# The expert loop of a two-block model: the next block's rows are transposed right behind the hidden transposes, inside the second down piece

## The chip, the cores and the metric

The kernel runs on one core of a Trainium2 chip. The metric is the device time of one execution in microseconds (us). The engines are TensorE (PE), VectorE (DVE), ScalarE (ACT), GpSimd (POOL) and SyncE (SP); each works through its own instructions in order, and they meet at semaphores: an instruction may add to a counter when it is done (`then_inc`), and an engine may wait until a counter has reached a value (`wait_ge`).

## The reference

The whole model is a state-space layer, an attention layer, a second block with two kinds of attention, and at its end a mixture of experts over 512 tokens of width 1024. The change lies in the experts:

```python
logits = h @ router_w + router_b          # 32 experts, the 4 best of each token
...
def expert_block(args):                   # 128 rows that go to one expert
    xe, e = args
    gate = jnp.minimum(xe @ w_gate[e] + b_gate[e], SWIGLU_LIMIT)
    up = jnp.clip(xe @ w_up[e] + b_up[e], -SWIGLU_LIMIT, SWIGLU_LIMIT)
    act = (up + 1) * (gate * jax.nn.sigmoid(SWIGLU_ALPHA * gate))
    return act @ w_down[e] + b_down[e]
yb = lax.map(expert_block, (xb, block_e))
```

Each expert has three matrices of 1024 x 1024 in float32. The rows' results are weighted and added up by token.

## The kernel before

**Blocks and pieces.** Tokens are packed into blocks of 128 rows of one expert. The number of blocks depends on the routing; here it is 35. A loop on each engine runs over all blocks but the last, which is written out behind it. A block reads 12 MB of weights, in 12 pieces of 1 MB (`PIECES`), q = 0 to 11: two gate pieces, two up pieces, again two gate and two up pieces for the second half of the hidden width, and four down pieces, q = 8 to 11.

**Exact products.** A float32 number is split into a high part that TensorE takes at full speed, and the low rest. A product is three matmuls: high by high, high by low, low by high (`exact_product`, L262 to L264). ACT makes the high part of each piece (`take_high`, L2988), DVE subtracts it from the raw piece to get the low part (`take_low`, L2992). There are four buffers for high parts, so ACT works `AHEAD` = 3 pieces ahead: in step q it waits until PE has used piece q - 1 (`used`), then rounds piece q + 3, which from q = 9 on is a piece of the next block.

**A block on PE.** PE waits for the block's rows (`x_ready`, L3133), takes pieces 0 to 7 (`open_products`, 12 matmuls of 512 columns each), and pieces 8 to 11 (`down_products`, 12 matmuls each: j = 0, 1 times two column halves times three). The inner activations come out of ACT and DVE with rows on the partitions; PE transposes them, four 128 x 128 transposes a half (`turn_hidden`, L3086): the first half behind piece 5, the second in the middle of piece 9. ACT and DVE then split them into high and low (L3198, L3266), and piece 10 waits for the second half's split (`hidden_split`).

**The next block's rows.** POOL gathers 128 rows of tokens into `x_rows` (`gather_rows`). PE transposes them by eight 128 x 128 transposes into banks 4 and 5 (`turn_rows`, L2973), ACT copies them out rounded (`take_x_high`, L2981), and DVE subtracts (`take_x_low`, L2984), which gives `x_ready`. In ACT's order the copy stands behind the rounding of step q = 10:

```python
for q in range(PIECES):
    of_piece(b, q, True)
    if q == 10:
        act.wait_ge(x_turned, b + 2)
        take_x_high()
```

DVE's order is alike: in step q it subtracts piece q + 3, and `take_x_low` stands behind step 10. In step 9 DVE has the hidden split (L3266) and the next block's piece 0, in step 10 the next block's piece 1.

SP loads the weight pieces in order; each load waits until PE has used the same piece of the block before.

Of the kernel before, what the change touches and what calls it, by code (L numbers as in the profile page):

```python
# [258 lines left out]
def exact_product(nc, out, left, right, start, stop):  # L259


    nc.tensor.matmul(out, left[0], right[0], start=start, stop=False)  # L262
    nc.tensor.matmul(out, left[0], right[1], start=False, stop=False)  # L263
    return nc.tensor.matmul(out, left[1], right[0], start=False, stop=stop)  # L264
# [2659 lines left out]
def experts(k, e, stored):  # L2924
# [32 lines left out]
    def number_left_out(engine):  # L2957
        return engine.value_load(plan[0:1, 2 * NP + 1:2 * NP + 2], min_val=0, max_val=NBLK - NE)

    def last_block(engine):  # L2960
        return engine.value_load(plan[0:1, 2 * NP + 2:2 * NP + 3], min_val=NE - 1, max_val=NBLK - 1)

    def block_number(engine, turn, left_out):
        return nc.s_assert_within(engine.snap((turn - left_out - 1) & 63), 0, NBLK - 2,
                                  skip_runtime_bounds_check_because="only turns above the number left out come here")
# [5 lines left out]
    def turn_rows():  # L2971
        for d in range(DT):
            i = nc.tensor.transpose(k.psum[:, 4 + d // 4, (d % 4) * P:(d % 4 + 1) * P], e["x_rows"][:, d * P:(d + 1) * P],  # L2973
                                    k.cst("ident"))
        i.then_inc(x_turned, 1)
# [18 lines left out]
    with nc.Block() as block:  # L2994
        @block.sync
        def _(sp):
            n = number_of_blocks(sp)
            with sp.Fori(1, NBLK) as b:
                with sp.If(b < n):
                    expert = sp.value_load(plan[0:1, bass.ds(b, 1)], min_val=0, max_val=NE - 1)  # L3000
                    for q in range(PIECES):

                        sp.wait_ge(used, PIECES * b + (q + 2 - PIECES))
                        load_expert_piece(k, e, sp, q, expert)
            sp.wait_ge(last_staged, 4)
            for t in range(ST):
                sp.dma_start(sums[:, t, :], k.sums_dram[t * P:(t + 1) * P, :]).then_inc(sums_in[t], 16)
            for c, t in units:
                if t == ST - 1:
                    sp.wait_ge(added_pool, c + 1)  # L3010
                else:
                    sp.wait_ge(added_dve, (ST - 1) * c + t + 1)
                sp.dma_start(k.io["out"][t * P:(t + 1) * P, c * NB:(c + 1) * NB], half(k.resid[:, t, :], c)).then_inc(stored, 16)
            sp.wait_ge(stored, 16 * len(units))
# [60 lines left out]
        @block.tensor  # L3075
        def _(pe):
            left_out = number_left_out(pe)
            pe.wait_ge(x_in, 16)
            nc.tensor.transpose(k.psum[:, 0, 0:P], k.cst("ident"), k.cst("ident")).then_inc(used, 1)
            turn_rows()  # L3080

            def turn_hidden(b, h):

                pe.wait_ge(hidden_ready, 2 * b + h + 1)
                for f in range(4):
                    i = nc.tensor.transpose(k.psum[:, 2 * h, f * P:(f + 1) * P], e["gate"][:, (4 * h + f) * P:(4 * h + f + 1) * P],  # L3086
                                            k.cst("ident"))
                i.then_inc(hidden_turned, 1)

            def open_products(b, q):  # L3090
                pe.wait_ge(low_ready, PIECES * b + (q + 1))
                r = q // 2
                w = [x.rearrange("p (d f) -> p d f", d=4) for x in (high[q % NHI], low[q])]
                for j in range(4):
                    d = 4 * (q % 2) + j
                    x = [t[:, d * P:(d + 1) * P] for t in (e["x_high"], e["x_low"])]
                    i = exact_product(nc, k.psum[:, r, :], x, (w[0][:, j, :], w[1][:, j, :]), start=(d == 0), stop=False)
                if q % 2 == 1:
                    if q == 1:
                        pe.wait_ge(chosen, b + 1)  # L3100
                    at = (r % 2) * D + (r // 2) * NB
                    i = nc.tensor.matmul(k.psum[:, r, :], e["choice"], e["bias"][:, at:at + NB], start=False, stop=True)  # L3102
                return i

            def down_product(q, j, c):
                f = 2 * (q - 8) + j
                x = [t[:, f * P:(f + 1) * P] for t in (e["hidden_high"], e["hidden_low"])]
                w = [x.rearrange("p (f c) -> p f c", f=2) for x in (high[q % NHI], low[q])]
                return exact_product(nc, k.psum[:, 6 + c, :], x, [t[:, j, c * NB:(c + 1) * NB] for t in w],
                                     start=(f == 0), stop=(f == DT - 1))  # L3110

            def down_waits(b, q):
                pe.wait_ge(low_ready, PIECES * b + (q + 1))
                if q == 8:
                    pe.wait_ge(y_ready, b + 1)
                if q % 2 == 0:
                    pe.wait_ge(hidden_split, 2 * b + ((q - 8) // 2 + 1))

            def down_products(b, q):
                down_waits(b, q)  # L3120
                for j in range(2):
                    for c in range(2):
                        i = down_product(q, j, c)
                    if q == 9 and j == 0:
                        turn_hidden(b, 1)
                return i

            with pe.Fori(0, NBLK // GROUP) as g:
                with pe.If(left_out < GROUP * g + (GROUP - 1)):
                    with pe.Fori(0, GROUP) as i:  # L3130
                        with pe.If(left_out < GROUP * g + i):
                            b = block_number(pe, GROUP * g + i, left_out)
                            pe.wait_ge(x_ready, b + 1)  # L3133
                            for q in range(8):
                                open_products(b, q).then_inc(used, 1)
                                if q == 5:
                                    turn_hidden(b, 0)
                            for q in range(8, PIECES):
                                down_products(b, q).then_inc(used, 1)
                                if q == 9:  # L3140
                                    pe.wait_ge(x_in, 16 * b + 32)
                                    turn_rows()

            last = last_block(pe)
            pe.wait_ge(x_ready, last + 1)
            for q in range(8):
                open_products(last, q).then_inc(used, 1)
                if q == 5:
                    turn_hidden(last, 0)
            for q in range(8, PIECES - 1):  # L3150
                down_products(last, q).then_inc(used, 1)
            down_waits(last, PIECES - 1)
            for c in range(2):
                for j in range(2):
                    i = down_product(PIECES - 1, j, c)
                i.then_inc(y_done, 1)

            def add_biases(c, t):
                for n in range(2):
                    at = n * D + c * NB  # L3160
                    nc.tensor.matmul(k.psum[:, bank_of(c, t), :], e["spread_t"][:, t * P:(t + 1) * P], e["bias"][:, at:at + NB],  # L3161
                                     start=(n == 0), stop=False)

            def spread_rows(c, t):
                to = e["onehot"][:, t * P:(t + 1) * P]
                nc.tensor.matmul(k.psum[:, bank_of(c, t), :], to, half(y_high, c), start=False, stop=False)
                nc.tensor.matmul(k.psum[:, bank_of(c, t), :], to, half(y_low, c), start=False, stop=True).then_inc(product, 1)

            for t in range(ST):
                add_biases(0, t)  # L3170
            pe.wait_ge(onehot_ready, ST)
            pe.wait_ge(y_low_ready, 1)
            for t in range(ST):
                spread_rows(0, t)
            for t in range(ST):
                if t >= 2:
                    pe.wait_ge(y_gated, t - 1)
                add_biases(1, t)
            pe.wait_ge(y_low_ready, 2)
            for t in range(ST):  # L3180
                spread_rows(1, t)
# [325 lines left out]
```

## Time and profile before

| | |
|---|---|
| median of 3 runs | 3100.88 us (3095.59 to 3105.14) |
| the profiled execution: its own time | 3099.18 us |
| its span in the trace | 3097.3 us |
| PE busy | 2926.6 us, 94% |
| DVE busy | 2052.1 us, 66% |
| ACT busy | 1593.9 us, 51% |
| expert loop, first to last row transposes | 1820.6 to 3028.6 us of the span |

The rows below are read as follows. Times are in us from the start of the span. A line such as L2988 is a line of the kernel. PE is matmuls, PEld is TensorE's weight loads. A matmul's end is modelled, so the distances of starts are what one reads on PE. "x4" is the number of instructions merged into a row. `[0.71 <-PE banks L264]` means that the engine was idle for 0.71 us and was released by PE's L264. The granted clock (PEclk) is 1.00 at 2.4 GHz and 0.50 at 1.2 GHz.

### The profile page before, as it was taken

The page shows a single profiled execution, that of the slowest core. Times are in us where ns is not written, and L with a number is a line of the kernel's source. Part 1 is how long each engine was busy: PE and PEld are TensorE (multiplying, and loading weights), DVE is VectorE, ACT ScalarE, POOL GpSimd, SP SyncE. Part 2 cuts the span into 40 slices and gives each one's busy share as a digit, 9 for nine tenths or more (in the row PEclk, how much of TensorE's full clock was granted, in tenths as well). Part 3 has the DMA queues.
Part 4 walks back from the last instruction along what each step waited for, and adds up shares of the span by engine and source line. Part 5 has one row for each costly group of instructions (what it writes and reads, how often), then busy time and mean ns, then how long its engine had stood idle before and what let it go on. Part 6 is the DMA issues. An engine that isn't in the chain of part 4 may idle for free. (4 is left out here: it accounts for less than half of the span.)

```text
span 3097.3 us, 42024 instructions
## 1 busy us (share of the span) xinstructions
PE 2926.6 (94%) x15072; PEld 2339.9 (76%) x15072; DVE 2052.1 (66%) x2363; ACT 1593.9 (51%) x1731; POOL 562.3 (18%) x480
## 2 busy tenths in 40 slices
PE   7889999997999999899999869999999999999997
PEld 3668888764688888776677768888888888888886
DVE  8451223657632236745653479999999999999998
ACT  4242222334632224434542247777777777777774
POOL 1002200021212100003101102332222322222225
PEclk9899999997999999999999879999999999999999
DMA  6512222212022322111013369999999999999994
GB/s 241 223 70 82 109 95 109 86 43 102 15 109 82 122 82 103 40 49 47 1 41 109 128 228 378 381 382 389 388 386 381 377 388 386 391 383 380 383 388 157
DMA packets 87918, 637.74 MB, mean 206 GB/s; under 512 B 10400, under 2 KB 10848, under 8 KB 25024
## 3 DMA queue, kind: packets, MB, share of 16 engines
q1 hardware_dynamic: 77584, 598.79, 49.6%
q0 software_dynamic: 9936, 36.75, 4.4%
q8 instruction: 77, 1.26, 0.2%
q10 hardware_dynamic: 288, 0.67, 0.1%
q14 instruction: 33, 0.27, 0.0%
HBM read 610.38 MB, written 25.79 MB: 205 GB/s over the span
## 5 line engine op out<-in xcount | busy, mean ns | idle before, releaser
L2992 DVE TENSOR_TENSOR arena_rounded<-arena,arena_rounded 128x2048 fp32r<-128x2048 f32 x420 | 960.9, 2309 | 94.5 <-ACT arena_rounded L2988 94.5
L2988 ACT ACTIVATE arena_rounded<-arena 128x2048 fp32r<-128x2048 f32 x420 | 801.5, 1918 | 210.4 <-PE banks L264 136.4
L262 PE MATMUL banks<-arena_rounded,operand_rounded 128*128 128x512 f32 (+1 forms) x2064 | 822.5, 399 | 14.0 <-DVE small_rounded L3266 8.1
L263 PE MATMUL banks<-arena_rounded,operand_rounded 128*128 128x512 f32 (+1 forms) x2064 | 806.2, 391 | 0.0
L264 PE MATMUL banks<-arena_rounded,operand_rounded 128*128 128x512 f32 (+1 forms) x1504 | 585.6, 389 | 0.0
L262 PEld LDWEIGHTS banks<-arena_rounded,operand_rounded 128*128 128x128 f32 x2064 | 391.3, 190 | 94.7 <-DVE arena_rounded L2992 8.9
L263 PEld LDWEIGHTS banks<-arena_rounded,operand_rounded 128*128 128x128 f32 x2064 | 391.4, 190 | 77.6 <-issue 1.0
L264 PEld LDWEIGHTS banks<-arena_rounded,operand_rounded 128*128 128x128 f32 x1504 | 284.5, 189 | 59.5
L262 PE MATMUL banks<-operand_rounded,arena_rounded 128*128 128x512 f32 (+2 forms) x712 | 267.2, 375 | 6.0 <-PE banks L264 5.3
L263 PE MATMUL banks<-arena_rounded,arena_rounded 128*128 128x512 f32 (+1 forms) x688 | 266.0, 387 | 0.0
L264 PE MATMUL banks<-operand_rounded,arena_rounded 128*128 128x512 f32 (+2 forms) x712 | 263.7, 370 | 0.0
L263 PE MATMUL banks<-operand_rounded,arena_rounded 128*128 128x512 f32 (+2 forms) x712 | 263.5, 370 | 0.0
L251 DVE TENSOR_TENSOR arena_rounded<-arena,arena_rounded 128x2048 fp32r<-128x2048 f32 x33 | 75.6, 2292 | 272.7 <-ACT arena_rounded L247 272.7
L262 PE MATMUL banks<-arena_rounded,arena_rounded 128*128 128x512 f32 (+1 forms) x608 | 236.6, 389 | 4.6 <-PEq L1369 2.3
L762 DVE TENSOR_TENSOR arena_rounded<-arena,arena_rounded 128x2048 fp32r<-128x2048 f32 x36 | 82.5, 2291 | 238.2 <-ACT arena_rounded L709 238.2
L264 PE MATMUL banks<-arena_rounded,arena_rounded 128*128 128x512 f32 (+1 forms) x608 | 235.1, 387 | 0.0
L264 PE MATMUL banks<-arena_rounded,small_rounded 128*128 128x512 f32 x560 | 220.7, 394 | 0.0
L709 ACT ACTIVATE arena_rounded<-arena 128x2048 fp32r<-128x2048 f32 x34 | 65.1, 1915 | 216.4 <-PE banks L264 212.1
L930 POOL TENSOR_TENSOR arena<-small 128x512 f32<-128x512 f32 x64 | 75.7, 1183 | 502.9 <-ACT small L916 257.5
L262 PEld LDWEIGHTS banks<-operand_rounded,arena_rounded 128*128 128x128 f32 (+1 forms) x712 | 133.8, 188 | 36.0 <-issue 13.6
L264 PEld LDWEIGHTS banks<-operand_rounded,arena_rounded 128*128 128x128 f32 (+1 forms) x712 | 133.8, 188 | 23.6
L263 PEld LDWEIGHTS banks<-operand_rounded,arena_rounded 128*128 128x128 f32 (+1 forms) x712 | 133.9, 188 | 23.4 <-issue 1.0
(493 smaller groups left out, 3969.0 us busy)
## 6 DMA issues: line engine op xcount, KB each, us to landing
arena<-in_gate SPq DMA_DIRECT2D x140, 1024.0 KB, 7.7
arena<-in_up SPq DMA_DIRECT2D x140, 1024.0 KB, 7.7
arena<-in_down SPq DMA_DIRECT2D x140, 1024.0 KB, 5.7
arena<-in_dense SPq DMA_DIRECT2D x62, 2048.0 KB, 7.7
arena<-in_dense SPq DMA_DIRECT2D x6, 1024.0 KB, 4.9
small<-in_rows SPq DMA_DIRECT2D x7, 512.0 KB, 7.5
expert_sums<-operand SPq DMA_DIRECT2D x5, 512.0 KB, 5.1
resid<-in_x SPq DMA_DIRECT2D x4, 512.0 KB, 6.8
```

The lines of the kernel that those rows point to most:

```text
L251: self.nc.vector.tensor_tensor(low, raw, high.bitcast(F32), ALU.subtract).then_inc(done, 1)
L262: nc.tensor.matmul(out, left[0], right[0], start=start, stop=False)
L263: nc.tensor.matmul(out, left[0], right[1], start=False, stop=False)
L264: return nc.tensor.matmul(out, left[1], right[0], start=False, stop=stop)
L709: nc.scalar.activation(w_high, raw, ACT.Copy).then_inc(high, 1)
L762: V.tensor_tensor(w_low, raw, w_high.bitcast(F32), ALU.subtract).then_inc(low, 1)
L930: nc.gpsimd.tensor_tensor(hidden[:, n, :], relu[:, n % 2, :], relu[:, n % 2, :], ALU.mult).then_inc(squared, 1)
L2988: nc.scalar.activation(high[q % NHI], raw[:, q, :], ACT.Copy).then_inc(high_ready, 1)
L2992: nc.vector.tensor_tensor(low[q], raw[:, q, :], high[q % NHI].bitcast(F32), ALU.subtract).then_inc(low_ready, 1)
```

## The change

The eight row transposes and the wait on the gathered rows are moved from behind piece 9 into its middle, right behind the four transposes of the hidden activations. The six matmuls of j = 1 of piece 9 now follow them. The last block, which has no next one, calls the same function without them.

```diff
-            def down_products(b, q):
+            def down_products(b, q, ahead):
                 down_waits(b, q)
                 for j in range(2):
                     for c in range(2):
                         i = down_product(q, j, c)
                     if q == 9 and j == 0:
                         turn_hidden(b, 1)
+                        if ahead:
+                            pe.wait_ge(x_in, 16 * b + 32)
+                            turn_rows()
                 return i
...
                             for q in range(8, PIECES):
-                                down_products(b, q).then_inc(used, 1)
-                                if q == 9:
-                                    pe.wait_ge(x_in, 16 * b + 32)
-                                    turn_rows()
+                                down_products(b, q, True).then_inc(used, 1)
...
-                down_products(last, q).then_inc(used, 1)
+                down_products(last, q, False).then_inc(used, 1)
```

The signal `used` of piece 9 hangs on the last matmul that the function returns. On PE, at the middle of piece 9 inside the loop, this is the first piece of the difference in PE's instructions; L3086 are the hidden transposes, L3127 is the wait on the gathered rows, L2973 the row transposes, L262 to L263 the first matmuls of j = 1:

```order
 L3084 REGISTER_ALU
 L3086 MATMUL banks<-const,operand 128x128 x4
+L3127 ISA
+L2973 MATMUL banks<-const,arena 128x128 x8
 L262 MATMUL banks<-arena_rounded_56,operand_rounded_49 128x512
 L263 MATMUL banks<-arena_rounded_54,operand_rounded_49 128x512
```

The row transposes came in ahead of the six matmuls of j = 1. At the end of piece 9 on PE, six matmuls on, they are gone; the last L264 shown carries the signal `used` in both kernels, and L3113 belongs to the first product of piece 10:

```order
 L263 MATMUL banks<-arena_rounded_54,operand_rounded_49 128x512
 L264 MATMUL banks<-arena_rounded_56,small_rounded_59 128x512
-L3141 ISA
-L2973 MATMUL banks<-const,arena 128x128 x8
 L3113 REGISTER_ALU
 L262 MATMUL banks<-arena_rounded_57,operand_rounded_49 128x512
```

The signal's matmul moved behind the transposes. The instructions of DVE, ACT, POOL and SP are the same in both kernels and stand in the same order.

## Rows read from the trace of the kernel before

**Rows 1.** The page: busy time, share of the span and instructions of each engine.
```profile
PE 2926.6 (94%) x15072; PEld 2339.9 (76%) x15072; DVE 2052.1 (66%) x2363; ACT 1593.9 (51%) x1731; POOL 562.3 (18%) x480
```

**Rows 2.** One turn of the loop: length, busy times, granted clock, DMA share, GB/s.
```profile
2389.08:2424.57 35.49, 35.49 (x166) 29.39 (x164) 32.80 (x22) 26.92 (x19) 9.80 (x7) 1.00 1.01 384
```

**Rows 3.** Waits in the expert stage: us in total, times, longest.
```profile
PE banks L262 <- DVE small_rounded L3266: 8.1, 2, 5.4
PE banks L262 <- DVE operand_rounded L2984: 3.1, 1, 3.1
...
DVE arena_rounded L2992 <- ACT arena_rounded L2988: 81.7, 99, 1.6
...
POOL expert_sums L3049 <- ACT operand L3229: 421.4, 34, 12.4
```

**Rows 4.** Row transposes; and who waited for DVE's L2984 (us, times).
```profile
L2973 PE MATMUL banks<-const,arena x280: 270/273/421, 1820.6 to 3028.6; 128*128 128x128 f32 x140
...
  PE banks L262: 3.1, 1
```

**Rows 5.** Timeline of PE in piece 9: start, duration, line, operation.
```profile
2422.50 0.40 PE L264 MATMUL banks<-arena_rounded,small_rounded 128*128 128x512 f32 x1
...
2423.41 0.39 PE L263 MATMUL banks<-arena_rounded,operand_rounded 128*128 128x512 f32 x1
...
2424.33 0.40 PE L264 MATMUL banks<-arena_rounded,small_rounded 128*128 128x512 f32 x1
...
2425.67 0.39 PE L263 MATMUL banks<-arena_rounded,operand_rounded 128*128 128x512 f32 x1
```

**Rows 6.** Timeline of ACT around the row copy L2981, and one earlier rounding.
```profile
2413.18 1.91 ACT L2988 ACTIVATE arena_rounded<-arena 128x2048 fp32r<-128x2048 f32 x1
...
2424.77 1.92 ACT L2988 ACTIVATE arena_rounded<-arena 128x2048 fp32r<-128x2048 f32 x1 [0.71 <-PE banks L264]
2426.59 1.01 ACT L2981 ACTIVATE operand_rounded<-banks 128x1024 fp32r<-128x1024 f32 x1
2428.39 1.92 ACT L2988 ACTIVATE arena_rounded<-arena 128x2048 fp32r<-128x2048 f32 x1 [0.79 <-PE banks L264]
```

**Rows 7.** Timeline of DVE around the row subtraction L2984, and one earlier subtraction.
```profile
2415.12 2.29 DVE L2992 TENSOR_TENSOR arena_rounded<-arena,arena_rounded 128x2048 fp32r<-128x2048 f32 x1 [0.50 <-ACT arena_rounded L2988]
...
2424.32 0.68 DVE L3266 TENSOR_TENSOR small_rounded<-banks,operand_rounded 128x512 fp32r<-128x512 f32 x1
2424.93 4.48 DVE L2992 TENSOR_TENSOR arena_rounded<-arena,arena_rounded 128x2048 fp32r<-128x2048 f32 x2
2429.33 1.21 DVE L2984 TENSOR_TENSOR operand_rounded<-banks,operand_rounded 128x1024 fp32r<-128x1024 f32 x1
```

**Rows 8.** Timeline at the border of two blocks.
```profile
2430.68 0.39 PE L264 MATMUL banks<-arena_rounded,small_rounded 128*128 128x512 f32 x1
2430.69 0.19 PEld L262 LDWEIGHTS banks<-arena_rounded,operand_rounded 128*128 128x128 f32 x1
...
2431.14 0.39 PE L263 MATMUL banks<-arena_rounded,operand_rounded 128*128 128x512 f32 x1
...
2431.19 0.69 ACT L3228 ACTIVATE operand<-banks,arena 128x512 f32<-128x512 f32 x1 [0.89 <-PE banks L264]
```

**Rows 9.** Timeline where PE really waited for DVE: before the loop, last block.
```profile
1824.13 1.23 DVE L2984 TENSOR_TENSOR operand_rounded<-banks,operand_rounded 128x1024 fp32r<-128x1024 f32 x1
...
1825.62 0.29 PEld L262 LDWEIGHTS banks<-arena_rounded,operand_rounded 128*128 128x128 f32 x1 [3.47 <-issue]
...
3073.64 0.68 DVE L3266 TENSOR_TENSOR small_rounded<-banks,operand_rounded 128x512 fp32r<-128x512 f32 x1
...
3074.44 0.19 PEld L262 LDWEIGHTS banks<-arena_rounded,operand_rounded 128*128 128x128 f32 x1 [3.11 <-DVE arena_rounded L2992]
...
3074.78 0.40 PE L263 MATMUL banks<-arena_rounded,operand_rounded 128*128 128x512 f32 x1
```

**Rows 10.** Busy times, clock after the 3.1 us wait (columns as in rows 2).
```profile
1825.00:1829.40 4.40, 3.78 (x9) 3.01 (x10) 2.14 (x2) 1.91 (x1) 1.28 (x3) 0.50 0.40 123
```

## The prediction

> **What bounds the kernel now.** I read the totals first, then the expert loop, then the waits in it, then one block instruction by instruction. The totals show TensorE (PE) busy 94% of the span and VectorE (DVE) 66% [rows 1], but that is an average over all stages. The edit touches only the expert loop, so I took one turn of it, from one set of row transposes to the next: 35.49 us, in which PE is busy all 35.49 us at a granted clock of 1.00, that is 2.4 GHz, and DVE 32.80 us [rows 2]. The list of waits says the same for the whole loop: from its first block on PE waited only three times, 3.1 us once (before the first block) and 8.1 us twice (in the last block) [rows 3]. In every turn between, PE ran one matmul behind the other, and DVE waited 81.7 us for ScalarE (ACT) [rows 3]. So PE sets the time, and a change can shorten the loop only by making PE's own stream shorter. It can lengthen it by making PE wait for something that so far came just in time. The reader should therefore look for what comes just in time.
>
> The row transposes run once before the loop and once in each of its 34 turns: 280 of them in eights are 35 sets [rows 4]. So whatever happens per turn counts 34 times; the 34th is what the last block's start waits for.
>
> **The part that only moves.** In the profiled turn the matmul before the four hidden transposes starts at 2422.50 and the second matmul behind them at 2423.41: 0.91 us. The same two points around the eight row transposes are 2424.33 and 2425.67: 1.34 us [rows 5]. Four more transposes cost 0.43 us, 0.108 each; eight added to a set that exists already cost 0.86 us, where a set of eight alone costs 1.34 - 0.46 = 0.88 (the 0.46 is two matmul pitches: 2431.14 - 2430.68 = 0.46, one 0.23 [rows 8]). Joining the two sets saves PE some 0.02 us a turn, 34 x 0.02 = 0.7 us in all, if nothing else happened. The wait on the gathered rows moves with them; it stands between two transposes now, where less work covers the instruction itself. No row shows a stand-alone wait between transposes. From below it is 0, which I take, since PE is fed ahead of its array; from above it is the 0.07 us that such a wait costs on ACT, whose L3228 starts 2431.19 - 2430.68 = 0.51 us behind the matmul that it waits for [rows 8], where a rounding without it starts 0.44 us behind (below). The gather itself is not late: GpSimd (POOL) comes to it in its own order, behind the 421.4 us that it waits for the block's output in the loop [rows 3], so that an earlier end of the transposes starts nothing earlier on it either.
>
> **The part that becomes late.** The signal that down piece 9 is used up goes with that piece's last matmul. Before, this matmul started at 2424.33, ahead of the row transposes; now the eight transposes stand ahead of its last six matmuls, so it starts 0.86 us later, at 2425.19. Follow who waits for it.
>
> ACT's rounding of the next block's second piece started at 2424.77, 0.44 us behind that matmul, and took 1.92 us [rows 6]. Now: 2425.19 + 0.44 = 2425.63, ending at 2427.55 in place of 2426.69. ACT's copy of the transposed rows (L2981) stands behind it in ACT's order. The transposes are ready earlier than before, but this copy starts later, about 2427.45 to 2428.46. ACT's next rounding started at 2428.39 [rows 6], behind an idle time, so ACT has caught up there.
>
> DVE's subtraction of that second piece is the second half of the pair that starts at 2424.93 and lasts 4.48 us. One takes 2.28, so the second started at 2427.13 [rows 7], 0.44 us after the rounding had ended: DVE had its own backlog, and this is the cover. The new end of the rounding, 2427.55, passes it. With the 0.03 us that DVE needs behind ACT (a rounding ended at 2413.18 + 1.91 = 2415.09 and the subtraction behind it started at 2415.12 [rows 6, 7]) the subtraction starts at 2427.58, 0.45 us later than before. DVE's row subtraction L2984 stands right behind it: it ran from 2429.33 to 2430.54 [rows 7] and now ends at 2430.99. Its own input from ACT, 2428.46, is in time.
>
> L2984 is what PE waits for at the head of each block. PE began to load that block's first weights at 2430.69, 0.01 us behind the start of the matmul before [rows 8], so nothing held it, but L2984 had ended only 0.15 us earlier. How long does PE need when it really waits? In the last block, DVE ended at 3073.64 + 0.68 = 3074.32 and PE loaded at 3074.44: 0.12 us; before the first block, for this very wait, DVE ended at 1825.36 and PE loaded at 1825.62: 0.26 us [rows 9]. The loop's own 0.15 us without a hold says that 0.12 to 0.15 is enough in the steady state, 0.26 being the upper bound. So of 0.45 us of lateness only 0 to 0.03 are covered.
>
> A late start gives something back. When PE restarts from idle, the second matmul came 3074.78 - 3074.44 = 0.34 us after the load [rows 9]; in the stream it is 2431.14 - 2430.69 = 0.45 [rows 8]. So 0.11 us are recovered. The new time of the second matmul is 2430.99 + 0.15 + 0.34 = 2431.48, against 2431.14: **0.34 us a turn**; with 0.12 it is 0.31, with 0.26 it is 0.45. PE's saving of 0.02 does not count any more, since PE waits at the end of this path anyway. The delay does not heal: the next block's chain on ACT and DVE is again started by PE's signals, and the 0.45 us arise anew.
>
> **The sum.** 34 x 0.34 = 11.6 us (0.31: 10.5; 0.45: 15.3). The profiled execution took 3099.18 us, its span 3097.3. 3099.2 + 11.6 = 3110.8. The median of the runs before, 3100.88, is 1.7 higher; from there it is 3112.5. I say 3112. With the moved wait exposed (0.07) on top it is 34 x 0.41 = 13.9, and with the 0.26 as well 34 x 0.52 = 17.7 us.
>
> A rule stands against holding the load back. The Trainium skill, page TensorE: Matmul & The Clock Gate, section Step-by-step: what each phase is for, says that TensorE pulls weight loads ahead of matmuls in flight. Here the weights are the rows that are late, and in [rows 9] the load starts at 1825.62, behind L2984's end and not ahead of it, so the trace shows no pull-ahead over the wait. By the rule the restart would save another 0.11 us a turn, and the sum would be about 8 us; its chance is part of the second rival's.
>
> **The rivals.**
> - *The cover holds, and only the saving is left* (not slower). One mechanism: DVE's backlog at piece 9 is longer in most turns than in the one I read, so that the rounding, though 0.86 us late, is still in time. It decides from 0.86 us of cover; the profiled turn has 0.44. For it: PE gets rid of one change between matmuls and transposes. Against it: L2984 never held PE in the loop [rows 4], and 34 turns without a wait of PE leave it little room to differ from one turn to the next. Time: 3099.2 - 0.7 = 3098.5 by the profile, 3100 by the median.
> - *Half the lateness is absorbed.* The 0.44 us from matmul to rounding shrinks, or the restart recovers more than 0.11. With 0 us from DVE's end to PE's load, the least that can be, the turn costs 2430.99 + 0.34 - 2431.14 = 0.19 us: 6.5 us, 3106 to 3107.
> - *The down pieces stall too.* The next wait of PE behind the set, for the split of the hidden rows, is met at 2424.32 + 0.68 = 2425.00 by DVE [rows 7]. PE's first load for that piece falls at 2425.20 now. 0.20 us is above the 0.12 us needed, by 0.08. If ACT or DVE slip by 0.2 us there, it costs 0.12 us x 34 = 4 us more: 3116.
> - *The short stops cost the clock.* PE would stand still once a turn for some 0.4 us. Before the first block PE was idle for 3.1 us and then ran 4.40 us at a granted clock of 0.50 (1.2 GHz) [rows 10]. If each stop did that, 34 x 2.2 = 75 us: 3174. The stops here are an eighth of that one, and the turn with its transposes runs at clock 1.00 throughout [rows 2]. The Trainium skill, same page, section A second HAM failure mode: psum-queue depth-cycling, names short idles between groups of matmuls as such a cause; no row of this kernel shows it for a stop this short.
>
> **How the numbers follow.** The head-of-block wait as summed: 0.70. Half absorbed: 0.10. Cover holds or nothing changes: 0.10. Down pieces stall too: 0.07. Clock: 0.03. The range 3104 to 3119 takes in the 3106 of the half-absorbed case and the 17.7 us of the upper bounds, and leaves out the holding cover and the clock. A measurement of this kernel tells about 0.3%, 9.3 us, from no change: 3110.2 is the border. My value lies only 2 us beyond it, so part of the likeliest case falls on this side. Slower: three quarters of 0.70, the down pieces, the clock: 0.63. Same: the rest of it and the two milder cases, less a little: 0.33. Faster: 0.04.
>
> **What would show it.** In the profile after, the turn is 35.8 to 35.9 us in place of 35.49; the list of waits shows PE waiting for DVE L2984 some 33 times more, in small pieces; ACT's idle time before the rounding ahead of L2981 is about 1.57 us in place of 0.71; DVE is idle some 0.4 us before the second subtraction of each pair; the set of twelve transposes is one piece on PE. If L2984 never appears as PE's releaser, the chain above is wrong. If it appears but for 0.1 us, the cover or the restart was mis-sized. If the granted clock is below 1.00 in the loop, the last rival has come true.

## The result and the profile after

The changed kernel's median is 3111.84 us over 13 runs; the kernel before, run beside it each time, has 3098.38 over 13. The ratio of the two is 1.0047, with a 95% interval of 1.0035 to 1.0058: slower, by 11 to 18 us. One of the changed kernel's thirteen runs took 3727.78 us at a mean granted clock of 0.74, where every other run of either kernel beside it lies at 3123.09 us or below; the ratio leaves it out, the median of the other twelve is 3111.0, and since it left no trace, whether the change has to do with it is not shown. The profiled execution has a span of 3108.3 us, against 3097.3.

The page of the changed kernel answers to [rows 1], and the row of one turn of the loop, here from one row subtraction L2984 to the next, to [rows 2]:

```profile
PE 2933.5 (94%) x15072; PEld 2337.3 (75%) x15072; DVE 2055.3 (66%) x2363; ACT 1593.1 (51%) x1731; POOL 577.6 (19%) x480
...
2434.13:2470.01 35.88, 35.77 (x166) 29.38 (x165) 32.90 (x22) 26.93 (x20) 10.47 (x7) 1.00 1.00 380
```

The turn went from 35.49 to 35.88 us with the same instructions and the clock still at 1.00. These are single turns. From here on "the turn" of a kernel is the mean distance of two starts of L2984 (L2985 where the lines are shifted) over the 33 turns behind the first: 35.87 us here, 35.49 before, 0.38 us more.

The timeline of the changed kernel, all engines, from the matmul ahead of the hidden transposes to the head of the next block (the answer to [rows 5 to 8]):

```profile
2426.83 0.40 PE L264 MATMUL banks<-arena_rounded,small_rounded 128*128 128x512 f32 x1
...
2427.06 0.60 PE L3086 MATMUL banks<-const,operand 128*128 128x128 f32 x4
...
2427.50 1.04 PE L2973 MATMUL banks<-const,arena 128*128 128x128 f32 x8
...
2428.61 0.39 PE L263 MATMUL banks<-arena_rounded,operand_rounded 128*128 128x512 f32 x1
2428.66 0.69 DVE L3266 TENSOR_TENSOR small_rounded<-banks,operand_rounded 128x512 fp32r<-128x512 f32 x1
...
2429.54 0.39 PE L264 MATMUL banks<-arena_rounded,small_rounded 128*128 128x512 f32 x1
...
2429.54 0.19 PEld L262 LDWEIGHTS banks<-arena_rounded,operand_rounded 128*128 128x128 f32 x1
...
2429.97 1.92 ACT L2988 ACTIVATE arena_rounded<-arena 128x2048 fp32r<-128x2048 f32 x1 [1.58 <-PE banks L264]
...
2431.79 1.01 ACT L2981 ACTIVATE operand_rounded<-banks 128x1024 fp32r<-128x1024 f32 x1
...
2431.92 2.29 DVE L2992 TENSOR_TENSOR arena_rounded<-arena,arena_rounded 128x2048 fp32r<-128x2048 f32 x1 [0.38 <-ACT arena_rounded L2988]
...
2434.13 1.22 DVE L2984 TENSOR_TENSOR operand_rounded<-banks,operand_rounded 128x1024 fp32r<-128x1024 f32 x1
...
2434.98 0.39 PE L264 MATMUL banks<-arena_rounded,small_rounded 128*128 128x512 f32 x1
...
2435.48 0.19 PEld L262 LDWEIGHTS banks<-arena_rounded,operand_rounded 128*128 128x128 f32 x1 [0.53 <-issue]
...
2435.82 0.40 PE L263 MATMUL banks<-arena_rounded,operand_rounded 128*128 128x512 f32 x1
```

Read it from the first row, 2426.83, as zero; before, the same point is 2422.50 [rows 5].

| behind the last matmul ahead of the hidden transposes, us | before | after | later by |
|---|---|---|---|
| last matmul of piece 9 (carries `used`) | 1.83 | 2.71 | 0.88 |
| ACT's rounding of the next block's second piece | 2.27 | 3.14 | 0.87 |
| DVE's subtraction of that piece | 4.63 | 5.09 | 0.46 |
| end of DVE's row subtraction L2984 | 8.04 | 8.52 | 0.48 |
| PE's load of the first weights of the next block | 8.19 | 8.65 | 0.46 |
| second matmul of the next block | 8.64 | 8.99 | 0.35 |

PE loads 0.13 us behind L2984's end, 0.50 us behind the start of the matmul before, where it was 0.01 us in [rows 8]. It does so at all 34 heads behind the first: the load stands 0.12 to 0.13 us behind L2984's end and 0.47 to 0.50 us behind the start of the matmul before. So the head of the block is where the time goes.

The rest of the 0.38 us is a slower start behind the hold: from the second matmul of the block to the first L3102, 23 matmuls on, it is 5.25 us here, 5.21 before; the medians over the 34 heads are 5.24 and 5.22. The far row in the changed kernel (the near one, 2435.82, stands above):

```profile
2441.07 0.39 PE L3102 MATMUL banks<-arena_rounded 128*128 128x512 f32 x1
```

And before, the row at the far end (the near one, 2431.14, is in [rows 8]):

```profile
2436.35 0.39 PE L3102 MATMUL banks<-arena_rounded 128*128 128x512 f32 x1
```

### The profile page after: what moved, and what is told of

It reads as the page before. It is cut to its first block and busy times, and to the rows that moved or that the text cites. A ratio compares the mean times of both kernels' runs of the same rounds, so it can differ in the third digit from the quotient of the medians.

```text
span 3108.3 us, 42024 instructions
## 1 busy us (share of the span) xinstructions
PE 2933.5 (94%) x15072; PEld 2337.3 (75%) x15072; DVE 2055.3 (66%) x2363; ACT 1593.1 (51%) x1731; POOL 577.6 (19%) x480
## 5 line engine op out<-in xcount | busy, mean ns | idle before, releaser
L262 PE MATMUL banks<-arena_rounded,operand_rounded 128*128 128x512 f32 (+1 forms) x2064 | 823.4, 399 | 18.3 <-DVE small_rounded L3266 8.4
L263 PE MATMUL banks<-arena_rounded,operand_rounded 128*128 128x512 f32 (+1 forms) x2064 | 806.1, 391 | 0.0
L264 PE MATMUL banks<-arena_rounded,operand_rounded 128*128 128x512 f32 (+1 forms) x1504 | 586.1, 390 | 0.0
L262 PEld LDWEIGHTS banks<-arena_rounded,operand_rounded 128*128 128x128 f32 x2064 | 391.0, 189 | 113.0 <-issue 25.6
L263 PEld LDWEIGHTS banks<-arena_rounded,operand_rounded 128*128 128x128 f32 x2064 | 391.4, 190 | 77.4 <-issue 1.0
L264 PEld LDWEIGHTS banks<-arena_rounded,operand_rounded 128*128 128x128 f32 x1504 | 284.6, 189 | 60.1
L262 PE MATMUL banks<-operand_rounded,arena_rounded 128*128 128x512 f32 (+2 forms) x712 | 267.9, 376 | 6.0 <-PE banks L264 5.2
L263 PE MATMUL banks<-arena_rounded,arena_rounded 128*128 128x512 f32 (+1 forms) x688 | 266.7, 388 | 0.0
L264 PE MATMUL banks<-operand_rounded,arena_rounded 128*128 128x512 f32 (+2 forms) x712 | 264.5, 371 | 0.0
L263 PE MATMUL banks<-operand_rounded,arena_rounded 128*128 128x512 f32 (+2 forms) x712 | 264.3, 371 | 0.0
L262 PE MATMUL banks<-arena_rounded,arena_rounded 128*128 128x512 f32 (+1 forms) x608 | 237.4, 390 | 4.6 <-PEq L1369 2.3
L264 PE MATMUL banks<-arena_rounded,arena_rounded 128*128 128x512 f32 (+1 forms) x608 | 235.6, 387 | 0.0
L264 PE MATMUL banks<-arena_rounded,small_rounded 128*128 128x512 f32 x560 | 219.9, 393 | 0.0
L262 PEld LDWEIGHTS banks<-operand_rounded,arena_rounded 128*128 128x128 f32 (+1 forms) x712 | 134.5, 189 | 35.9 <-issue 13.6
L264 PEld LDWEIGHTS banks<-operand_rounded,arena_rounded 128*128 128x128 f32 (+1 forms) x712 | 134.6, 189 | 23.5
L263 PEld LDWEIGHTS banks<-operand_rounded,arena_rounded 128*128 128x128 f32 (+1 forms) x712 | 134.6, 189 | 23.4 <-issue 1.0
```

## The experiments

The theory: the signal `used` of piece 9 is late, so ACT's rounding is late, so DVE's subtraction is late beyond its cover of 0.44 us, so L2984 behind it is late, and PE holds. The first rival: the new place costs PE itself (twelve transposes in a row, a switch in the middle of piece 9, the wait between transposes). The second: ACT's late row copy L2981 holds L2984.

### Only the rounding is late

PE's instructions are those of the kernel before, in the same order. Only ACT changes:

```diff
                             for q in range(PIECES):
+                                if q == 10:
+                                    act.wait_ge(x_turned, b + 2)
                                 of_piece(b, q, True)
                                 if q == 10:
-                                    act.wait_ge(x_turned, b + 2)
                                     take_x_high()
```

> The kernel before, with its row transposes at their old place and TensorE's instructions untouched; only ScalarE now waits for the end of the row transposes ahead of its rounding of the next block's second piece, where it waited for the end of piece 9. If the lateness of this rounding is the cause: the rounding starts 0.98 us later (0.75 us from the start of a set of four transposes to ScalarE's answer, 0.43 more for eight, against 0.20 after their start before), DVE's row subtraction ends 0.57 us later, and the turn grows by 0.43 us at the block's head and some 0.03 in the matmuls behind the restart, to 35.95 us; 34 turns give about 15 us, 3113 to 3115. If the place of the transposes on TensorE is the cause (twelve in a row, or the wait between them), the turn stays at 35.49 us and the time at that of the kernel before.

Measured: 3116.36 us median over 5 runs, against 3096.25 over 15 of the kernel before, ratio 1.0064 (1.0050 to 1.0077); turn 36.00 us, 0.05 above what was expected: the row subtraction came 0.6 us late in place of 0.57, and the rounding 1.01 in place of 0.98. The timeline of this kernel at the same places:

```profile
2394.45 0.40 PE L264 MATMUL banks<-arena_rounded,small_rounded 128*128 128x512 f32 x1
...
2397.73 1.92 ACT L2988 ACTIVATE arena_rounded<-arena 128x2048 fp32r<-128x2048 f32 x1 [1.71 <-PE banks L2973]
...
2399.69 2.29 DVE L2992 TENSOR_TENSOR arena_rounded<-arena,arena_rounded 128x2048 fp32r<-128x2048 f32 x1 [0.52 <-ACT arena_rounded L2988]
2401.90 1.22 DVE L2984 TENSOR_TENSOR operand_rounded<-banks,operand_rounded 128x1024 fp32r<-128x1024 f32 x1
...
2403.24 0.19 PEld L262 LDWEIGHTS banks<-arena_rounded,operand_rounded 128*128 128x128 f32 x1 [0.64 <-issue]
...
2403.25 0.49 PE L262 MATMUL banks<-arena_rounded,operand_rounded 128*128 128x512 f32 x1 [0.22 <-DVE operand_rounded L2984]
```

The rounding starts 3.28 us behind the reference point (the last matmul ahead of the hidden transposes, here 2394.45), 1.01 later than before, and PE's first load comes 0.12 us behind L2984's end at 2403.12. A wait on ACT alone, with the transposes where they were, makes the turn longer by more than the change does, 0.51 against 0.38 us. The first rival falls as the main cause. In this kernel the list of PE's waits names L2984 in every turn:

```profile
PE banks L262 <- DVE operand_rounded L2984: 10.6, 35, 3.1
```

### The rows ahead of the rounding and the subtraction

The changed kernel; the transposes stay in the middle of piece 9, and ACT and DVE take the rows first. On DVE, and alike on ACT:

```diff
                             for q in range(PIECES):
-                                of_piece(b, q, True)
                                 if q == 10:
                                     dve.wait_ge(x_high_ready, b + 2)
                                     take_x_low()
+                                of_piece(b, q, True)
```

> The changed kernel, with ScalarE's row copy ahead of the rounding of the next block's second piece, and DVE's row subtraction ahead of its subtraction of that piece. If the chain used, rounding, subtraction, row subtraction is the cause: the row subtraction ends some 2 us before TensorE needs it, the head of a block has no hold, and the turn is 35.48 us, TensorE's own stream; time as before the change, within 0.1%. If the place of the transposes costs TensorE itself, the turn stays at 35.87 us and the time near 3112.

Measured: 3096.76 us median over 11 runs, against the same 3096.25, ratio 0.9998 (0.9989 to 1.0007); turn 35.46 us. The whole loss is gone with the twelve transposes in place. Timeline of this kernel:

```profile
2421.84 0.40 PE L264 MATMUL banks<-arena_rounded,small_rounded 128*128 128x512 f32 x1
...
2423.59 1.03 ACT L2981 ACTIVATE operand_rounded<-banks 128x1024 fp32r<-128x1024 f32 x1 [0.17 <-PE banks L2973]
2424.98 1.92 ACT L2988 ACTIVATE arena_rounded<-arena 128x2048 fp32r<-128x2048 f32 x1 [0.37 <-PE banks L264]
...
2426.48 1.22 DVE L2984 TENSOR_TENSOR operand_rounded<-banks,operand_rounded 128x1024 fp32r<-128x1024 f32 x1
2427.61 2.28 DVE L2992 TENSOR_TENSOR arena_rounded<-arena,arena_rounded 128x2048 fp32r<-128x2048 f32 x1
```

L2984 ends 5.86 us behind the reference point, where PE's load of [rows 8] stands at 8.19. The rounding is as late as in the changed kernel (3.14), and it does no harm: what costs the time is the row subtraction that stood behind it.

### Four or six of the eight transposes in the middle

```diff
-                            turn_rows()
+                            turn_rows(0, 4)
...
                                 down_products(b, q, True).then_inc(used, 1)
+                                if q == 9:
+                                    turn_rows(4, DT)
```

> The changed kernel with four of the eight row transposes in the middle of piece 9 and four behind it. The signal of piece 9 is 0.43 us late and DVE's cover is 0.44 us: by the chain the second subtraction starts at most 0.02 us later, the head has no hold, the turn is 35.49 to 35.52 us. If what counts is that transposes stand in the middle at all (the wait, the switch), the turn grows by at least half of 0.38, to 35.68.

> The changed kernel with six of the eight row transposes in the middle of piece 9 and two behind it. By the chain: 0.65 us late less 0.44 of cover and plus 0.03 gives 0.25 us at the row subtraction, of which the spare 0.02 and the 0.11 of the restart go off: 0.11 us at the head, 0.03 behind it, turn 35.61 to 35.63 us. If the cost goes with the number of transposes moved, three quarters of 0.38: 35.77 us.

Measured, one run each: turn 35.51 us and 3100.14 us with four; turn 35.64 us and 3103.21 us with six. The 15 runs of the kernel before beside them reach from 3093.23 to 3103.74, so these two are read by their turns and not by their times. In both, these lines are one number on (L2989 is the rounding, L2993 the subtraction, L2985 the row subtraction). With four:

```profile
2422.90 0.40 PE L264 MATMUL banks<-arena_rounded,small_rounded 128*128 128x512 f32 x1
...
2425.60 1.92 ACT L2989 ACTIVATE arena_rounded<-arena 128x2048 fp32r<-128x2048 f32 x1 [1.12 <-PE banks L264]
...
2425.34 4.51 DVE L2993 TENSOR_TENSOR arena_rounded<-arena,arena_rounded 128x2048 fp32r<-128x2048 f32 x2
2429.76 1.22 DVE L2985 TENSOR_TENSOR operand_rounded<-banks,operand_rounded 128x1024 fp32r<-128x1024 f32 x1
```

DVE's two subtractions are still one piece: the cover has just held. L2985 ends 8.08 us behind the reference point, 0.04 later than before, which uses up PE's spare time; the turn is 0.02 us longer. With six there is a gap of 0.15 us, and a hold:

```profile
2423.95 0.40 PE L264 MATMUL banks<-arena_rounded,small_rounded 128*128 128x512 f32 x1
...
2426.87 1.92 ACT L2989 ACTIVATE arena_rounded<-arena 128x2048 fp32r<-128x2048 f32 x1 [1.35 <-PE banks L264]
...
2428.82 2.29 DVE L2993 TENSOR_TENSOR arena_rounded<-arena,arena_rounded 128x2048 fp32r<-128x2048 f32 x1 [0.15 <-ACT arena_rounded L2989]
...
2432.37 0.19 PEld L262 LDWEIGHTS banks<-arena_rounded,operand_rounded 128*128 128x128 f32 x1 [0.26 <-issue]
```

All kernels in which ACT and DVE keep their order give one curve of the turn over the start of the rounding behind the reference point:

| kernel | rounding starts at | turn |
|---|---|---|
| before | 2.27 | 35.49 |
| four in the middle | 2.70 | 35.51 |
| six in the middle | 2.92 | 35.64 |
| the change (eight) | 3.14 | 35.87 |
| before, rounding held on ACT | 3.28 | 36.00 |

It is nearly flat up to 2.70, and from 2.92 on it rises by 0.23 in 0.22 us and by 0.13 in 0.14: one for one. A cost that goes with the number of transposes moved would have put four of them at 35.68 and six at 35.77.

### One side at a time, and the wait

Only ACT's copy ahead, or only DVE's subtraction ahead, by the half of the edit above that belongs to it:

> The changed kernel with only ScalarE's row copy moved ahead of the rounding of the next block's second piece; DVE's order as it was. The copy fits into ScalarE's idle time of 1.58 us, the rounding still starts when piece 9 is used up, DVE still subtracts that piece first: the turn stays at 35.87 us. If instead the late row copy (0.8 us later than before the change) is what holds the row subtraction, the turn falls back to 35.49.

> The changed kernel with only DVE's row subtraction moved ahead of its subtraction of the next block's second piece; ScalarE's order as it was. The row copy ends about 5.97 us behind the last matmul ahead of the hidden transposes, the row subtraction 1.25 us later, 1 us before TensorE needs it: no hold, turn 35.48 us. If the ScalarE side is the bound, the turn stays at 35.87 us.

Measured: with ACT alone, turn 35.87 us, one run of 3107.71 us; with DVE alone, turn 35.46 us, one run of 3095.52 us, where a single run of the kernel before beside both took 3100.53. Here too the turns decide. The rows of DVE with ACT's order alone changed:

```profile
2430.87 2.29 DVE L2992 TENSOR_TENSOR arena_rounded<-arena,arena_rounded 128x2048 fp32r<-128x2048 f32 x1 [0.38 <-ACT arena_rounded L2988]
2433.08 1.22 DVE L2984 TENSOR_TENSOR operand_rounded<-banks,operand_rounded 128x1024 fp32r<-128x1024 f32 x1
```

and with DVE's order alone changed:

```profile
2429.03 1.23 DVE L2984 TENSOR_TENSOR operand_rounded<-banks,operand_rounded 128x1024 fp32r<-128x1024 f32 x1 [1.28 <-ACT operand_rounded L2981]
2430.17 2.28 DVE L2992 TENSOR_TENSOR arena_rounded<-arena,arena_rounded 128x2048 fp32r<-128x2048 f32 x1
```

In the second, DVE stands idle for 1.28 us for the late row copy, and still L2984 ends 0.93 us ahead of PE's load. In the first, the copy starts 1.74 us behind the reference point in place of 4.96, and nothing is gained. The second rival falls: the copy is not what holds L2984, DVE's own order is, through the subtraction that must wait for the rounding.

Last, the wait on the gathered rows, moved ahead of the hidden transposes, with both row steps first:

```diff
                     if q == 9 and j == 0:
+                        if ahead:
+                            pe.wait_ge(x_in, 16 * b + 32)
                         turn_hidden(b, 1)
                         if ahead:
-                            pe.wait_ge(x_in, 16 * b + 32)
                             turn_rows()
```

> Both row steps ahead, as in the kernel with both moved, and the wait on the gathered rows ahead of the hidden transposes, so that no wait stands between the twelve. Compared with the turn of that kernel it shows what the wait costs TensorE: expected 0.00 to 0.02 us a turn, at most 0.07.

Measured: turn 35.46 us with the wait at either place, one run of 3095.49 us. The wait between transposes costs nothing that can be read.

## Why the prediction was right, step by step

- **What bounds the loop.** Right: PE's stream set the turn, and in the kernels without a hold it does so again, at 35.46 us.
- **The part that only moves.** Forecast: 0.02 us a turn saved by joining the sets. Measured with the hold taken away: 35.49 - 35.46 = 0.03. Worth 1 us in the whole, below what the runs can tell (0.9998, 0.9989 to 1.0007). The moved wait cost 0, the lower bound that was taken.
- **The signal and the rounding.** Forecast 0.86 us late; measured 0.88 and 0.87.
- **The cover.** Forecast 0.44 of 0.86, leaving 0.45 with the 0.03 for DVE's answer; measured 0.46. The kernel with four in the middle, put at this edge, and the one with six show the edge where it was said to be.
- **PE's answer.** 0.12 to 0.15 us was taken, with the 0.26 from before the first block as upper bound. Measured 0.12 to 0.13 at every head; the 0.26 did not come up in the loop. It had been read where the granted clock was 0.50 [rows 10], and at that place the changed kernel took 0.40 (L2984 ends at 1822.53, the load stands at 1822.93).
- **The recovery of 0.11 at the restart.** Measured: load 0.46 later, second matmul 0.35. The restart distance from load to second matmul is 0.34, as in [rows 9]. The Trainium skill (TensorE: Matmul & The Clock Gate, Step-by-step: what each phase is for) says that TensorE pulls weight loads ahead of matmuls in flight, and says nothing of waits. Here the load stands behind L2984's end at every head, so none was pulled ahead across this wait, and the further 0.11 us that the prediction worked out by the rule did not come.
- **The size.** 0.34 us a turn was forecast, 0.35 is what the head shows, and 0.38 is the turn. The term that was missing is the slower pitch behind the restart, 0.02 us in the median and 0.04 in the turn shown. 34 x 0.38 = 12.9 us, within the measured 11 to 18. Forecast 3112, measured 3111.84, or 3111.0 over the twelve runs. That they lie so close is partly luck: the forecast stood on the 3100.88 of three runs, where thirteen gave 3098.38, and its 11.6 us were too small by 1 to 2, so that two errors ran against each other.
- **What would show it.** One sign was named wrongly. I wrote that PE's list of waits would name L2984 some 33 times more and that the chain is wrong if it never does. In the changed kernel's list the loop adds nothing to the one wait before the first block:

```profile
PE banks L262 <- DVE operand_rounded L2984: 3.1, 1, 3.1
```

A matmul's end is modelled: the last one of a block starts at 2434.98 and is drawn 0.39 us long, the next is drawn from 2435.48, so a gap of 0.11 is left, and most of the hold lies under the drawn end; the timelines and lists of waits here show no idle time below 0.15. In the kernel with the rounding held, PE's load stands 0.60 us behind the start of the matmul before, in place of 0.50; the drawn gap is 0.22, and the list has the wait 35 times, at 10.6 us in total. So the absence of L2984 from the list did not speak against the chain. The signs that did hold are distances of starts, and DVE's 0.38 and ACT's 1.58 us of idle time.
- **The rivals.** The down pieces did not stall: L3266 ends at 2429.35, 0.19 us ahead of PE's load for piece 10 at 2429.54, and the matmuls go on at 0.23. The clock stayed at 1.00 in every turn of the profiled execution behind the first. The price of this last rival was misread, too: [rows 10] does not show a clock that falls at a stop, since in the same execution the granted clock was 0.50 already ahead of the 3.1 us wait and all through it:

```profile
1817.00:1825.00 8.00, 2.18 (x9) 1.78 (x9) 7.57 (x4) 4.99 (x4) 1.55 (x3) 0.50 0.20 70
```

The profiled span grew by only 11.0 us. The first row subtraction stands at 1824.1 us before and 1821.3 after, the last at 3032.6 and 3043.8: the loop itself grew by 14.0, and the stages ahead of it, which are the same in both kernels, happened to end 2.8 us earlier. Of the 14.0, 33 turns of 0.38 are 12.5; the rest lies in the first turn (below).

## What to carry to other kernels

Before moving work on the busiest engine, look at which signal goes with the last instruction of the piece it is moved into: everything ahead of that instruction delays the signal, even if the engine's own stream gets no longer. A stage that never waits can still have its input arriving 0.02 us before it would; read that spare time from the producer's end to the consumer's load, and subtract it from the lateness that you make. When work is made ready earlier, move its consumers ahead too: the transposed rows were ready 1.4 us earlier and were copied 0.9 us later, because ACT and DVE kept them behind work that had become late. Here DVE's order decided: changing it alone took the whole loss away, changing ACT's alone took none.

## What the hardware showed that was not expected

Behind a head at which PE had waited for L2984, the next 23 matmuls took some 0.02 us longer than in the stream, at clock 1.00: 5.24 us in the median, against 5.22 before and in every kernel without a wait. It is 5.24 with four transposes in the middle as well, where the wait itself costs about 0.01 us. So it does not grow with the hold; what makes it is not shown.

When the first block begins, the clock is still 0.50. Rows of the windows, after, then before, then with DVE's order alone changed (columns as in rows 2):

```profile
1825.00:1829.00 4.00, 4.00 (x10) 3.09 (x10) 2.18 (x1) 0.55 (x1) 0.00 (x0) 0.50 0.22 90
1829.00:1833.00 4.00, 4.00 (x19) 3.23 (x18) 2.29 (x1) 2.60 (x3) 0.00 (x0) 1.00 0.85 270
```

```profile
1825.00:1829.00 4.00, 3.38 (x8) 2.71 (x9) 1.74 (x2) 1.91 (x1) 1.28 (x3) 0.50 0.44 135
1829.00:1833.00 4.00, 4.00 (x17) 3.23 (x17) 1.45 (x2) 1.92 (x1) 0.00 (x0) 0.93 0.35 76
```

```profile
1825.00:1829.00 4.00, 3.42 (x8) 2.76 (x9) 1.66 (x2) 1.91 (x1) 1.20 (x3) 0.50 0.42 135
1829.00:1833.00 4.00, 4.00 (x13) 3.11 (x13) 0.81 (x1) 1.90 (x1) 0.00 (x0) 0.65 0.19 27
```

The changed kernel began at 1822.93 and ran 6.1 us at the low clock, the kernel before at 1825.62 and ran 4.0. The 2.1 us more at half rate explain some 1.1 us of the first turn, 38.97 against 37.39 us; the 0.38 is the other part. This is no effect of the change that could be told from chance: the kernel with DVE's order alone changed began at 1825.58 and ran 6.2 us at the low clock, and over the nine kernels' traces that stretch lies anywhere between 3.4 and 6.2 us. A difference of an us or so between two profiled spans can come from there.
